# All sixteen gate tiles of a hybrid mLSTM and state-space layer computed in its state-space stage

## The chip, the cores and the metric

The kernel runs on one core of a Trainium2 chip. The core has five engines, each with its own instruction stream, that meet only at semaphores: TensorE (PE, matmuls; PEld is its loading of weights), VectorE (DVE), ScalarE (ACT), GpSimd (POOL) and SyncE (SP), the last two used here mostly to start transfers (DMAs). The metric is the device time of one execution in microseconds (us), as the median of several runs. The times in the rows come from one execution that was recorded by the hardware profiler.

## What is computed

One layer of a diffusion backbone runs over 512 latent tokens and 128 context tokens (640 in all, width 1024). A combined projection feeds an mLSTM (4 heads of width 256, two directions), a state-space branch (S5, 32 groups of 16 channels) and two gates `ga` and `gb`. The two branches are merged under the gates, and a mixture of 16 experts follows. What matters here, cut from the reference:

```python
proj = h @ p['w_in']
q, k, v, o, gates, u, ga, gb = jnp.split(proj, IN_SPLITS, axis=-1)
...
merged = jax.nn.sigmoid(ga) * (h_a @ p['w_pA']) + jax.nn.sigmoid(gb) * (h_b @ p['w_pB'])
out = merged @ p['w_out']
```

`ga` and `gb` are 2048 columns in all. The kernel computes `sigmoid(ga)` and `sigmoid(gb)` as sixteen tiles of 128 columns by 640 tokens.

## The kernel before

The program is a row of stages, each a block in which every engine has its instructions written out in order; at the end of a block all engines meet. The stages are: input and modulation, small projections, the state-space stage, its gated output, the mLSTM, the merge with the output projection, the router, the experts.

**A gate tile.** Tile u is made by `pe_gate` (lines 232 to 241): PE waits for its weights and for the sigmoid of tile u - 1, then runs eight pairs of matmuls, each pair 512 latent and 128 context columns wide (L239, L240), into two PSUM banks. `act_gate` (243 to 249) has ACT take the sigmoid of both banks into a staging row (L248, L249). `store_gate` (251 to 256) has POOL store the row to DRAM (L254) and, behind every odd tile, load the half of the gate weights that comes two halves later (L229). A half is 1 MB and serves two tiles; there are eight halves in two buffers, which are the free tile xT. The merge reads the stored tiles back.

**Where the tiles are.** `NU_S5` (L223) says that tiles 0 to 12 belong to the state-space stage and 13 to 15 to the mLSTM.

**The state-space stage** (blocks up to L950) runs over four quarters q of 8 groups. PE's order is written by hand (L772 on, loop from L776): `lags(q)`, a turn of modulation rows (`pe_ada_turn`, L198), a gate, modulation rows (`pe_ada_rows`, L191), a gate, the coefficients of the next quarter turned (`turn_cb`, L717), a gate, `additions(q + 1, 0)` (L729), `outputs(q)` (L763, L765), `additions(q + 1, 1)`, modulation rows. One more gate stands ahead of the loop. ACT follows in the same order: it copies what PE leaves in PSUM (additions L823 to L826, outputs L864, modulation rows L208, lags L838, turned coefficients L812) and takes the sigmoids between. DVE computes the scan of each quarter (L919 to L944) and the coefficients of the next (L511 to L534).

**The mLSTM** runs over four heads h. PE's order (L1171 on) is `scores(h)` (L1101 to L1116), the projection of the next head's q and k, `values(h)` (L1133, L1143), the projection of the next head's v and o, `turn(h)` (transposes L1155, state update L1166). The last head has no next one; there PE computes tiles 13 and 14 in the first of these places and tile 15 in the second. Beside PE, ACT computes decays (L1216 to L1228), sigmoids, the scaled parts of the values (`inter`, L1237) and, in `finish`, a square root (L1242) and copies; DVE multiplies scores by decays (`weigh`, L1294), combines the values (`combine`, L1303 to L1319), forms the inverse mean square (L1323) and scales the head by its root (L1326), for which PE's transposes wait. Values wait until all five products L1294 are done.

When ACT changes to a function whose table is not loaded, an instruction ACT_TABLE_LOAD stands in front of the activation and bears its line.

Of the kernel before, what the change touches and what calls it, by code (L numbers as in the profile page):

```python
# [27 lines left out]
H, DH = 4, 256  # L28
# [44 lines left out]
def program(nc, ar, out):  # L73
    with ExitStack() as ctx:
# [145 lines left out]


        NU = 16
        NU_S5 = 13  # L223
        gw = xT[:].rearrange("p k t -> p (k t)")[:, 0:4096].rearrange("p (s k n) -> p s k n", s=2, k=KD)
        gstage = [xT[:].rearrange("p k t -> p (k t)")[:, 4096:4096 + TOK], rsb[:]]

# [435 lines left out]
        with ExitStack() as st:  # L662
# [41 lines left out]
            @block.tensor  # L704
            def _(pe):
                gates = iter(range(NU_S5))

                def turn_cb(q, r):

                    if r == 0:  # L710
                        pe.wait_ge(sem("cb_ready"), q + 1)
                        if q:
                            pe.wait_ge(sem("v_copied"), 4 * q)
                    else:
                        pe.wait_ge(sem("ct_copied"), 4 * q + 2)
                    for g in range(QG):
                        mm = pe.transpose(PS[2 + g // 4][:, (g % 4) * P:(g % 4 + 1) * P], CB[:, r, g, :], ident)  # L717
                        if g % 4 == 3:
                            mm.then_inc(sem("cb_turned"), 1)

                def additions(q, r):

                    if r == 0:
                        pe.wait_ge(sem(f"part_in{q}"), 16 * L)
                        pe.wait_ge(sem("ct_copied"), 4 * q + 4)
                    else:
                        pe.wait_ge(sem("v_copied"), 4 * q + 2)
                    for g in range(QG):
                        mm = pe.matmul(PS[2 + g // 4][:, (g % 4) * J:(g % 4 + 1) * J], CT[:, r, g, :],  # L729
                                       U[:, QG * q + g, :], start=True, stop=True)  # L730
                        if g % 4 == 3:
                            mm.then_inc(sem("s5_v_done"), 1)

                def lags(q):

                    pe.wait_ge(sem("ca_ready"), q + 1)
                    pe.wait_ge(sem("bbz_ready"), q + 1)
                    if q:
                        pe.wait_ge(sem("lags_copied"), 4 * q)
                    FW, BW = (L - 1) * GC, 0  # L740
                    for s in range(2):
                        o = s * (2 * L - 1) * GC
                        k = 0
                        for d, (at, m0) in enumerate(((FW, 0), (BW, 1))):
                            for r in range(2):
                                for x in range(4):
                                    g = 4 * s + x
                                    mm = pe.matmul(PS[6][32 * x:32 * x + GC, o + at:o + at + P], bbz[:, d, r, g, :],
                                                   CA[:, r, g, m0:m0 + L, :], start=(k == 0 and s == 0),
                                                   stop=(k == 3), skip_group_check=True)  # L750
                                k += 1
                    mm.then_inc(sem("s5_lag_done"), 1)

                def outputs(q):

                    pe.wait_ge(sem("xp_copied"), q + 1)
                    pe.wait_ge(sem("cao_ready"), q + 1)
                    pe.wait_ge(sem("toeplitz_in"), 128 * (q + 1))
                    if q:
                        pe.wait_ge(sem("z_copied"), 2 * q)  # L760
                    for g in range(QG):
                        dst = PS[g // 4][0:J, (g % 4) * P:(g % 4 + 1) * P]
                        pe.matmul(dst, U[:, QG * q + g, :], T[:, g, :], start=True, stop=False)  # L763
                        for r in range(2):
                            mm = pe.matmul(dst, Xp[:, r, g, :], CAo[:, r, g, :], start=False, stop=(r == 1))  # L765
                        if g % 4 == 3:
                            mm.then_inc(sem("s5_y_done"), 1)

                def gate():
                    pe_gate(pe, next(gates), (4, 5))  # L770

                turn_cb(0, 0)  # L772
                turn_cb(0, 1)
                gate()
                additions(0, 0)
                for q in range(NQ):  # L776
                    lags(q)
                    if q:
                        pe_ada_turn(pe, 3 + 2 * q, 7)
                    else:  # L780
                        additions(0, 1)
                    gate()
                    pe.wait_ge(sem("mod_in"), 4 + 2 * q)
                    pe_ada_rows(pe, 4 + 2 * q, 7)
                    gate()
                    if q + 1 < NQ:
                        turn_cb(q + 1, 0)
                    pe_ada_turn(pe, 4 + 2 * q, 7)
                    if q + 1 < NQ:
                        turn_cb(q + 1, 1)  # L790
                    gate()
                    if q + 1 < NQ:
                        additions(q + 1, 0)
                    outputs(q)
                    if q + 1 < NQ:
                        additions(q + 1, 1)
                    pe.wait_ge(sem("mod_in"), 5 + 2 * q)
                    pe_ada_rows(pe, 5 + 2 * q, 7)
                pe_ada_turn(pe, 11, 7)

            @block.scalar
            def _(act):
# [12 lines left out]
                def additions(q, r):  # L815

                    if q and r == 0:
                        act.wait_ge(sem("xp_copied"), q)
                    for b in range(2):
                        act.wait_ge(sem("s5_v_done"), 4 * q + 2 * r + b + 1)  # L820
                        src = PS[2 + b][:, 0:4 * J].rearrange("p (g j) -> p g j", g=4)
                        gg = slice(4 * b, 4 * b + 4)
                        act.activation(V[F, r, gg, 1:JL + 1], src[F, :, 0:JL], ACT.Copy)  # L823
                        act.activation(V[F, r, gg, JL + 2:NS_], src[F, :, JL:J], ACT.Copy)
                        act.activation(V[B, r, gg, 1:JL + 1], src[B, :, 0:JL][:, :, ::-1], ACT.Copy)
                        act.activation(V[B, r, gg, JL + 2:NS_], src[B, :, JL:J][:, :, ::-1],  # L826
                                       ACT.Copy).then_inc(sem("v_copied"), 1)
# [5 lines left out]
                for q in range(NQ):  # L833
# [27 lines left out]
                    for b in range(2):  # L861
# [3 lines left out]
                                       PS[b][0:J, :].rearrange("p (g i c) -> p g i c", g=4, i=L),  # L865
                                       ACT.Copy).then_inc(sem("z_copied"), 1)
                    if q + 1 < NQ:
                        additions(q + 1, 1)
                    act_ada(act, 5 + 2 * q, 7)

# [143 lines left out]
        with ExitStack() as st:  # L1014
            qk = sb("qk", [P, 2, 4, TOK], F32, st)
# [32 lines left out]
            @block.gpsimd  # L1048
            def _(pool):
                for h in range(H):  # L1050
                    pool.wait_ge(sem("co_ready"), 4 * (h + 1))
                    for d in range(2):
                        pool.dma_start(Cout[h, d], Co[:, 2 * d:2 * d + 2, :]).then_inc(sem("c_out"), 16)
                    if h == H - 2:
                        for u in range(NU_S5, NU):
                            store_gate(pool, u, qk[:, 0, u % 2, :])
                pool.wait_ge(sem("c_out"), 32 * H)

            @block.tensor
            def _(pe):  # L1060
# [110 lines left out]
                for h in range(H):  # L1171
                    scores(h)
                    if h + 1 < H:
                        proj_qk(h + 1)
                    else:
                        for u in range(NU_S5, NU - 1):
                            pe_gate(pe, u, (u % 2, 2))
                    values(h)
                    if h + 1 < H:
                        proj_vo(h + 1)  # L1180
                    else:
                        pe_gate(pe, NU - 1, ((NU - 1) % 2, 2))
                    turn(h)

            @block.scalar
            def _(act):
# [71 lines left out]
                for h in range(H):  # L1258
                    decays(h)
                    if h + 1 < H:  # L1260
                        out_qk(h + 1)
                    else:
                        for u in range(NU_S5, NU - 1):
                            act_gate(act, u, (u % 2, 2), qk[:, 0, u % 2, :])
                    inter(h)
                    if h + 1 < H:
                        out_vo(h + 1)
                    else:
                        act_gate(act, NU - 1, ((NU - 1) % 2, 2), qk[:, 0, (NU - 1) % 2, :])
                    finish(h)  # L1270

            @block.vector
# [718 lines left out]
```

## Time and profile before

| What | Value |
|---|---|
| median of 3 runs | 1861.05 us (1856.96 to 1862.49) |
| profiled execution | 1856.57 us, of which the recorded span is 1854.7 us |
| PE busy | 1689.7 us (91%) |
| DVE busy | 570.0 us (31%) |
| ACT busy | 374.7 us (20%) |
| POOL busy | 100.4 us (5%) |
| mean granted clock of PE over the span | 0.962 |

All times in the rows count from the start of the span. The granted clock is the share of PE's full speed that the chip allowed: 1.00 is 2.4 GHz, 0.50 is 1.2 GHz, and a value between is a stretch that had both. The state-space stage lies between some 110 and 300 us, the mLSTM between 337 and 804, its last head from 733, the merge from 807. A busy PE is not PE at its best; it says only that its instructions follow without a wait.

### The profile page before, as it was taken

Reading aid. Unit: us, or ns where it says so; the run is one execution under the profiler, and the core shown is the slowest. Engines: PE = TensorE matmul, PEld = TensorE weight load, DVE = VectorE, ACT = ScalarE, POOL = GpSimd, SP = SyncE. Lnnn points to the kernel's source line nnn. Section 1 sums busy time; section 2 is a strip of 40 time slices with the busy share of each in tenths; the row PEclk is TensorE's granted clock in tenths of the full one; section 3 lists DMA queues with packets and bytes.
Section 4 is the critical chain, followed back from the end, with each engine's and each line's share of the span. In section 5 each row is a group of like instructions: output and inputs, shape, how many; then the busy total and the mean of one; then the engine's idle time right before and its main releaser. Section 6 shows DMA issues by size and latency. Waiting matters only on the chain. (4 is left out here: it accounts for less than half of the span.)

```text
span 1854.7 us, 33663 instructions
## 1 busy us (share of the span) xinstructions
PE 1689.7 (91%) x15258; PEld 960.7 (52%) x15258; DVE 570.0 (31%) x1313; ACT 374.7 (20%) x777; POOL 100.4 (5%) x95
## 2 busy tenths in 40 slices
PE   5799998999999898968995699999999999999993
PEld 2366665546446464668883234444444444444441
DVE  5369991011213131347646001111111111111113
ACT  3343332121121313145434100000000000000001
POOL 1610000000000000000000000000000000000000
PEclk9799998999999999989998799999999999999997
DMA  9244455010202012043314799999999999999963
GB/s 396 77 110 169 154 182 230 12 46 1 102 12 103 11 47 79 15 157 123 139 69 193 277 355 384 403 401 402 400 403 405 408 404 404 406 400 405 407 255 128
DMA packets 56916, 420.61 MB, mean 227 GB/s; under 512 B 10932, under 2 KB 17588, under 8 KB 26948
## 3 DMA queue, kind: packets, MB, share of 16 engines
q1 hardware_dynamic: 49188, 386.97, 52.7%
q0 software_dynamic: 6864, 28.85, 5.2%
q8 instruction: 120, 1.97, 0.4%
q10 hardware_dynamic: 720, 2.62, 0.3%
q14 instruction: 24, 0.20, 0.0%
HBM read 391.86 MB, written 24.42 MB: 224 GB/s over the span
## 5 line engine op out<-in xcount | busy, mean ns | idle before, releaser
L1737 PE MATMUL bank<-place,x 128*32 128x384 f32 x3120 | 258.1, 489 | 0.9 <-ACT x L1800 0.9
L1737 PE MATMUL bank<-ring_tail,x 128*32 128x384 f32 x3024 | 249.8, 488 | 1.4 <-issue 1.4
L1737 PEld LDWEIGHTS bank<-place,x 128*32 128x32 f32 x3120 | 100.4, 110 | 147.3 <-issue 143.8
L1737 PEld LDWEIGHTS bank<-ring_tail,x 128*32 128x32 f32 x3024 | 98.2, 110 | 145.1 <-issue 143.8
L1831 DVE SCALAR_TENSOR_TENSOR hT<-bank,gvr,xT 32x256 f32<-32x256 f32 (+1 forms) x192 | 92.1, 480 | 241.3 <-PE bank L1767 238.7
L1845 DVE TENSOR_TENSOR hid<-sq,bank 128x384 f32<-128x384 f32 x48 | 23.7, 550 | 446.8 <-issue 362.3
L1089 PE MATMUL bank<-place,hT 128*128 128x512 f32 x320 | 138.0, 592 | 0.0
L239 PE MATMUL bank<-hT,xT 128*128 128x512 f32 x256 | 132.7, 600 | 1.1 <-ACT qk L249 0.9
L1767 PE MATMUL bank<-place,hidT 128*32 128x256 f32 x2304 | 128.0, 379 | 0.0
L1767 PE MATMUL bank<-ring_tail,hidT 128*32 128x256 f32 x2304 | 127.8, 379 | 0.0
L1438 PE MATMUL bank<-a_h,w_h 128*128 128x320 f32 x320 | 101.2, 316 | 19.4 <-DVE w_l L1510 16.9
L1074 PE MATMUL bank<-hT,place 128*128 128x512 f32 x256 | 110.6, 592 | 2.5 <-PEq L952 2.5
L1767 PEld LDWEIGHTS bank<-place,hidT 128*32 128x32 f32 x2304 | 74.0, 110 | 51.3 <-issue 5.0
L1767 PEld LDWEIGHTS bank<-ring_tail,hidT 128*32 128x32 f32 x2304 | 74.3, 110 | 50.7 <-issue 3.3
L1438 PE MATMUL bank<-a_l,w_h 128*128 128x320 f32 x320 | 99.8, 312 | 0.0
L1438 PE MATMUL bank<-a_h,w_l 128*128 128x320 f32 x320 | 99.6, 311 | 0.0
L1089 PEld LDWEIGHTS bank<-place,hT 128*128 128x128 f32 x320 | 60.7, 190 | 74.8 <-issue 74.6
L1818 ACT ACTIVATE hidT<-bank 128x384 f32<-128x384 f32 x48 | 20.1, 491 | 363.6 <-PE bank L1751 363.6
L240 PEld LDWEIGHTS bank<-hT,xT 128*128 128x128 f32 x256 | 48.8, 191 | 61.7 <-issue 61.7
L1074 PEld LDWEIGHTS bank<-hT,place 128*128 128x128 f32 x256 | 48.3, 190 | 62.0 <-issue 62.0
L1438 PEld LDWEIGHTS bank<-a_h,w_h 128*128 128x128 f32 x320 | 60.9, 190 | 22.2 <-DVE w_l L1510 18.1
L1699 POOL DMA_INDIRECT moe_dram<-hT,gidx x16 | 23.1, 1442 | 741.9 <-DVE hT L1831 741.9
(364 smaller groups left out, 1905.4 us busy)
## 6 DMA issues: line engine op xcount, KB each, us to landing
place<-w_e_dram SPq DMA_DIRECT2D x97, 1536.0 KB, 11.6
ring_tail<-w_e_dram SPq DMA_DIRECT2D x95, 1536.0 KB, 11.7
place<-w_ada_dram SPq DMA_DIRECT2D x12, 2048.0 KB, 9.1
xT<-w_gate_dram POOLq DMA_DIRECT2D x8, 1024.0 KB, 6.5
place<-w_qk_dram SPq DMA_DIRECT2D x4, 2048.0 KB, 8.9
place<-w_vo_dram SPq DMA_DIRECT2D x4, 2048.0 KB, 10.7
place<-w_pAB_dram SPq DMA_DIRECT2D x4, 1536.0 KB, 7.9
hT<-gates_dram SPq DMA_DIRECT2D x4, 1280.0 KB, 6.1
```

The costliest lines, as they stand in the source:

```text
L239: pe.matmul(PS[banks[0]][:, :], w, hT[:, k, 0:LAT], start=(k == 0), stop=(k == 7))
L240: mm = pe.matmul(PS[banks[1]][:, 0:CTX], w, hT[:, k, LAT:TOK], start=(k == 0), stop=(k == 7))
L1074: mm = pe.matmul(PS[u % 2][:, :], w, hT[:, k, 0:LAT], start=(k == 0), stop=(k == 7))
L1089: mm = pe.matmul(PS[u % 2][:, :], hT[:, k, t * P:(t + 1) * P], wslot(c)[:, k, :], start=(k == 0), stop=(k == 7))
L1438: mm = pe.matmul(PS[bank][:, 0:TH], wp[:, n % RING, j * P:(j + 1) * P], ap[:, n % RING, x * TH:(x + 1) * TH], start=(k == 0 and i == 0), s ...
L1699: pool.indirect_dma_start(out=ar["moe"][:, :], out_offset=bass.IndirectOffsetOnAxis(ap=gidx[:, e:e + 1], axis=0), in_=ys[:, e % 2, :], in_ ...
L1737: mm = pe.matmul(PS[bank + j][TJ * g:TJ * g + TJ, 0:FC], x[:, e % 2, 2 * c + k, TJ * j:TJ * j + TJ], w[:, k, FC * g:FC * g + FC], start=(c ...
L1767: mm = pe.matmul(PS[y_bank(e) + j // 2][TJ * g:TJ * g + TJ, 256 * (j % 2):256 * (j % 2) + 256], hidT[:, e % 2, j, b * P + TJ * c:b * P + T ...
L1818: ins = act.activation(hidT[:, e % 2, j, :], PS[j][:, 0:FC], ACT.Copy)
L1831: ins = dve.scalar_tensor_tensor(ys[TJ * j:TJ * j + n, e % 2, 256 * g:256 * g + 256], PS[y_bank(e) + j // 2][TJ * g:TJ * g + n, 256 * (j % ...
L1845: ins = dve.tensor_tensor(hid[:, j, :], sl[:, j, :], PS[3 + j][:, 0:FC], ALU.mult)
```

## The change

All sixteen tiles are computed in the state-space stage: `NU_S5` becomes 16, and one more gate stands, on PE and on ACT, behind the outputs of the first, second and third quarter, ahead of the second additions of the next. These three are tiles 4, 8 and 12; the tiles between keep their places and take other numbers. The last mLSTM head loses its three gates on PE and ACT, and POOL its three stores there.

```diff
-        NU_S5 = 13
+        NU_S5 = 16
...
                     outputs(q)
                     if q + 1 < NQ:
+                        gate()
                         additions(q + 1, 1)
                     pe.wait_ge(sem("mod_in"), 5 + 2 * q)
...
                                        ACT.Copy).then_inc(sem("z_copied"), 1)
                     if q + 1 < NQ:
+                        gate()
                         additions(q + 1, 1)
                     act_ada(act, 5 + 2 * q, 7)
...
-                    if h == H - 2:
-                        for u in range(NU_S5, NU):
-                            store_gate(pool, u, qk[:, 0, u % 2, :])
...
                     if h + 1 < H:
                         proj_qk(h + 1)
-                    else:
-                        for u in range(NU_S5, NU - 1):
-                            pe_gate(pe, u, (u % 2, 2))
                     values(h)
                     if h + 1 < H:
                         proj_vo(h + 1)
-                    else:
-                        pe_gate(pe, NU - 1, ((NU - 1) % 2, 2))
                     turn(h)
...
                     if h + 1 < H:
                         out_qk(h + 1)
-                    else:
-                        for u in range(NU_S5, NU - 1):
-                            act_gate(act, u, (u % 2, 2), qk[:, 0, u % 2, :])
                     inter(h)
                     if h + 1 < H:
                         out_vo(h + 1)
-                    else:
-                        act_gate(act, NU - 1, ((NU - 1) % 2, 2), qk[:, 0, (NU - 1) % 2, :])
                     finish(h)
```

## Rows read from the trace of the kernel before

**Rows 1.** Busy time by stretch, one state-space quarter: us, PE, PEld, DVE, ACT, POOL; PEclk, DMA, GB/s

```profile
219.98:264.34 44.36, 44.19 (x307) 29.57 (x306) 40.72 (x92) 17.13 (x39) 3.05 (x5) 1.00 0.53 175
```

**Rows 2.** Waits of PE (125.7 to 301) and DVE (175 to 301): total us, times, longest

```profile
PE bank L717 <- ACT place L812: 0.5, 3, 0.2
...
DVE modT L212 <- PE bank L198: 6.8, 4, 3.7
DVE Kt L914 <- ACT Kt L838: 3.5, 3, 1.2
```

**Rows 3.** Timeline of PE, state-space stage: start, us, line, out<-in, count

```profile
131.29 1.06 PE L239 MATMUL bank<-hT,xT 128*128 128x512 f32 x2
...
140.08 1.92 PE L191 MATMUL bank<-place,cs 128*32 128x512 f32 x16
...
168.82 0.60 PE L765 MATMUL bank<-place,sq 128*80 128x128 f32 x4
169.26 1.91 PE L729 MATMUL bank<-U,place 128*128 128x80 f32 x16
...
174.70 1.05 PE L198 MATMUL bank<-sel,adar 128*128 128x2 f32 x8
...
197.98 1.02 PE L239 MATMUL bank<-hT,xT 128*128 128x512 f32 x2
...
206.63 1.91 PE L729 MATMUL bank<-U,place 128*128 128x80 f32 x16
```

**Rows 4.** Timeline of ACT behind the outputs of the first quarter; idle time in brackets

```profile
170.31 0.38 ACT L823 ACTIVATE place<-bank 64x256 f32<-64x256 f32 x1 [0.26 <-PE bank L729]
...
173.09 0.60 ACT L208 ACTIVATE adar<-bank 128x512 f32<-128x512 f32 x1 [0.78 <-PE bank L191]
```

**Rows 5.** Timeline of DVE, its first instruction on the second quarter's additions

```profile
184.69 0.84 DVE L919 TENSOR_TENSOR tz<-place 128x656 f32<-128x656 f32 x1
```

**Rows 6.** The page's DMA issues: count, KB each, median us to landing

```profile
xT<-w_gate_dram POOLq DMA_DIRECT2D x8, 1024.0 KB, 6.5
```

**Rows 7.** Timeline of PE in the last mLSTM head

```profile
744.32 0.61 PE L1116 MATMUL bank<-qk 128*128 128x128 f32 x4
...
763.25 1.03 PE L1133 MATMUL bank<-C,qk 128*128 128x257 f32 x4
...
780.49 0.70 PE L1143 MATMUL bank<-vt,Pm 128*128 128x257 f32 x2 [0.32 <-DVE nd L1303]
...
789.46 0.38 PE L240 MATMUL bank<-hT,xT 128*128 128x128 f32 x2
793.66 2.36 PE L1155 MATMUL bank<-consts,hacc 128*128 128x128 f32 x10 [3.81 <-DVE hacc L1326]
...
798.07 2.37 PE L1166 MATMUL bank<-vt,place 128*128 128x257 f32 x8 [1.63 <-DVE place L1330]
```

**Rows 8.** Timeline of DVE in the last mLSTM head

```profile
744.52 1.28 DVE L1294 TENSOR_TENSOR Pm<-Pm,bank 128x128 f32<-128x128 f32 x4 [0.83 <-PE bank L1113]
...
786.33 0.19 DVE L1323 RECIPROCAL ssq<-ssq 128x5 f32<-128x5 f32 x1
792.20 1.40 DVE L1326 TENSOR_SCALAR hacc<-hacc,rs 128x256 f32<-128x256 f32 x5 [5.69 <-ACT rs L1242]
```

**Rows 9.** Timeline of ACT in the last mLSTM head

```profile
733.26 1.28 ACT L1223 ACT_TABLE_LOAD   x1
737.48 0.40 ACT L1223 ACTIVATE Pm<-sq,colT 128x128 f32<-128x128 f32 x1 [2.93 <-DVE sq L1282]
...
790.66 1.28 ACT L1242 ACT_TABLE_LOAD   x1
```

**Rows 10.** Busy time by stretch in the last head, columns as in rows 1

```profile
733.30:744.80 11.50, 11.50 (x29) 5.49 (x30) 4.62 (x12) 8.09 (x20) 1.42 (x2) 0.85 0.14 47
...
753.40:754.50 1.10, 0.18 (x2) 0.01 (x1) 0.00 (x0) 0.77 (x2) 0.00 (x0) 1.00 0.00 0
...
795.00:796.00 1.00, 1.00 (x6) 1.00 (x5) 0.00 (x0) 0.99 (x4) 0.00 (x0) 0.50 0.00 0
```

## The prediction

> **What bounds the kernel now.** On the page TensorE (PE) is the busiest engine, but that is a mean over stages with different limits, so I read it stage by stage, and only the two stages that the change touches.
>
> First the busy time by stretch over one quarter of the state-space stage. The reader is to see a quarter of 44.36 us with PE busy for 44.19 of it and VectorE (DVE) for 40.72, at a granted clock of 1.00 [rows 1]. Two engines are nearly full, so the next view asks which waits for which. In the list of waits PE's largest entry is 0.5 us in three waits on ScalarE (ACT), while DVE waits 6.8 us in four for PE's line 198 and 3.5 us in three for the lag tables that follow PE's lags [rows 2]. So **PE is the bound of a quarter**, with DVE some 2 us behind.
>
> Then the timeline of PE, DVE and ACT in the last mLSTM head, where the other three gate tiles are now. The reader is to see three places: PE's first values matmul at 763.25, its transposes at 793.66, and what each was waiting for [rows 7 to 9]. Around them the head's path is scores, DVE's weighing, values, DVE's combining, ACT's square root, DVE's scaling, transposes.
>
> **The state-space stage: three gates more.** A gate is eight pairs of matmuls. The one at 197.98 is followed by additions at 206.63: 8.65 us [rows 3]. The one at 131.29 is followed by other work at 140.08: 8.79 us [rows 3]. The new gates stand between the outputs (last matmul group at 168.82) and the second additions (169.26) [rows 3], where PE now stands still for nothing, so nothing there hides them. I take the row that is also followed by additions: 3 x 8.65 = **+25.95 us**, with 3 x 8.79 = 26.37 as the upper end. PE's waits in this stage could at most vanish, which puts the lower end 0.5 lower, at 25.4.
>
> Does a new wait come with them? Everything behind the new gate moves together by 8.65, so I look at what runs beside it.
> - ACT gets two sigmoids between its copies of the outputs and its copies of the second additions. The gate's PE wait on the sigmoid before it is long met, since a whole set of outputs lies between. The copies of the additions start at 170.31, 1.05 behind the additions at 169.26, and ACT's copy of the modulation row starts behind them at 173.09, while PE asks for that row at 174.70 [rows 3, 4]. The existing gate at 197.98 has the same neighbours (sigmoids, then copies of additions) and PE does not wait there. Cost taken: nothing; without this cover a sigmoid pair late by its own length, some 0.9 us, in each of three quarters.
> - DVE takes the additions up only at 184.69 [rows 5], 11 us behind ACT's last copy, so it does not notice. DVE's other work of the quarter gets 8.65 us more room.
> - GpSimd (POOL) stores each tile and, behind odd tiles, loads the weights two halves ahead. A half lands in a median of 6.5 us [rows 6], and two whole gates, 17.3 us, lie between its request and its use. The new tiles are numbers 4, 8 and 12, even ones, so in their places only a store is added; the odd ones keep gates on both sides. SyncE's weight loads wait for the same PE steps as before. Cost taken: nothing.
>
> **The last head: three gates less.** Two lie between scores and values. The scores end at 744.32 + 0.61 = 744.93 [rows 7]. Values need all five products of DVE; the last ends at 744.52 + 1.28 = 745.80 [rows 8]. From DVE's end to PE's start I take what the transposes show: scaling ends at 792.20 + 1.40 = 793.60, PE starts at 793.66, so 0.06 [rows 7, 8]. Values then start at 745.86 instead of 763.25: **17.39 us gained** of the two gates' 18.3 or so; what is late next is DVE's last product, 0.93 us behind the scores. If DVE's end were not the last, the scores' end would be the limit, 0.93 better.
>
> The third gate follows the values (last group at 780.49, ending 781.19) and ends at 789.46 + 0.38 = 789.84 [rows 7]. It is on the path for another reason: ACT must do its sigmoids, then load the square root's table (790.66, 1.28 us), before DVE scales at 792.20, although DVE had the mean squares ready at 786.33 + 0.19 = 786.52 [rows 8, 9]. Without it that table is loaded behind ACT's last copy for the values, while DVE still combines: a table load does not wait for its operand, as the one at 733.26 shows, 4.2 us ahead of the first exponential at 737.48 [rows 9]. DVE then scales 0.06 + 0.26 = 0.32 behind 786.52, where 0.06 is the handoff above and 0.26 is 792.20 less the table load's end at 791.94: 786.84. That is **5.36 us gained**; with the table load in the way, 4.08.
>
> Together 22.75 us; ends 17.39 + 4.08 = 21.5 and 22.75 + 0.93 = 23.7. So of three gates (25.95 us) just some 3.2 us was ever hidden in the head, and 22.75 stood on its path. The modules behind it (copies of the state, its store, the merge) follow in the same order.
>
> Here the Trainium skill speaks against the change: "Perfetto Trace Analysis", section Optimization Strategy, says that where the most-contended engine changes from stage to stage, interleaving the stages may pay, which means keeping filler where PE waits for others. By it the three gates were free and the sum would be +26; by the rows above it is +3.2.
>
> **The clock.** PE now stands still from 789.84 to 793.66, and the clock is already 0.50 for the transposes [rows 7, 10]. Afterwards it stands still from 763.80 to about 770.9 (both ends shifted by their gains), 7.1 us. The transposes cost the same, since they are at half clock today. The eight state-update matmuls behind them take 2.37 us [rows 7]. Should the clock still be down for them too, they lose between nothing and their own length, 2.4 us; I take **+0.4**, near to nothing, because a part of that time is waits for ACT to copy the first four away. Ahead of the values the wait is 0.93 us. In the run of before, between the first two gates of this head, PE was busy for only 0.18 of 1.10 us and the clock stayed at 1.00 [rows 10].
>
> **Sum.** +25.95 - 22.75 + 0.4 = **+3.6 us**; ends +25.4 - 23.7 = +1.7 and +26.37 - 21.5 + 2.4 = +7.3. The profiled execution took 1856.57 us (span 1854.7), so it would become 1860.2; it lies 4.5 us under the median of the three runs. On the median the forecast is 1861.05 + 3.6 = **1864.6**.
>
> **Rivals.**
> - *The values run cold (slower).* The scores of this head spent part of their time at half clock: 0.85 over 11.5 us is 2 x 0.15 x 11.5 = 3.45 us at half [rows 10]. The gates behind them are dense work. Values without them could meet another such stretch: half of 3.45 lost, 1.7 us, giving 1866.4; two stretches give 1868.1; all 17.9 us at half give +18, 1882. It decides from 2.0 us lost, 4 us at half more than today. For it: the longer standstill behind, and a clock that fell in this head already. Against: the scores end and the values begin at 1.00, and 0.92 us without work left it there. The Trainium skill ("TensorE: Matmul & The Clock Gate", section on HAM oscillation) says that a PE that pauses between bursts of work falls to half rate and pays when it returns; the turn of the head agrees (0.50), the short wait does not.
> - *A quarter gets a new wait (slower).* If sigmoids, store or a weight load came late in each of three quarters, 0.9 to 2 us each: +2.7 to +6, 1867 to 1871. Against: the slack of 1.6 us or more in each row above.
> - *The gates of the head were free after all (slower).* +26, 1887. It needs something other than DVE's product at 745.80 to hold the values; I see none.
> - *The quarters hide gates (faster).* Were PE's row padded and DVE the true bound, a quarter of DVE's 40.72 plus its short gaps could take in a gate. One of three hidden gives 1856, still about equal; two give 1847. For it: DVE's load. Against: DVE waits for PE in every quarter, not the reverse [rows 2].
> - *The change does nothing in the head*, values starting no earlier: the same +26 as above.
>
> **How the numbers follow.** About 0.3%, 5.6 us, is what a measurement of this kernel can tell from no change. Forecast, within that: 0.68. Cold values or turn beyond it: 0.19; new waits: 0.07; free gates: 0.01; hidden gates: 0.05. So faster 0.05, same 0.68, slower 0.27. The range takes the low end of the sum on the lower runs, 1856.96 + 1.7 = 1858.7, and reaches up past its high end on the median, 1868.4, to the two cold stretches and the new waits: 1858.5 to 1870.
>
> **What would show it.** Each of the first three quarters 8.65 us longer, PE without a wait over 0.5 us in it; values of the last head about 1 us behind the scores; a square-root table load ahead of the mean squares; transposes some 25 us behind the first values matmul (before: 30.4); the merge about 3.6 us later than now. Wrong would be a PE wait behind a new gate, or a granted clock under 0.9 while the values run.

## The result, and the profile after

The changed kernel takes 1873.17 us (median of 7 runs, 1868.9 to 1879.47) against 1861.05 (7 runs, 1856.96 to 1869.51): ratio 1.0066, 95% interval 1.0041 to 1.009. It is **slower by 12.1 us**, where +3.6 was forecast. The profiled execution took 1870.34 us (before: 1856.57).

Where the difference lies, from the two profiled executions:

| Stretch | before, us | after, us | difference | forecast |
|---|---|---|---|---|
| start to the first gate | 116.3 | 116.7 | +0.4 | 0 |
| first gate to the mLSTM's first projection | 221.0 | 247.8 | +26.8 | +25.95 |
| from there to the last head's scores | 396.0 | 399.0 | +3.0 | 0 |
| last head, start of its scores to its transposes | 60.4 | 37.6 | -22.7 | -22.75 |
| transposes to the merge's first matmul | 15.9 | 17.2 | +1.3 | +0.4 |
| merge | 155.5 | 160.4 | +4.8 | 0 |
| the rest | | | +0.2 | 0 |

The two large terms came out as forecast. Some 9 us came from three stretches whose work the change does not touch. The view of busy time by stretch shows what differs in them (us, then busy us of PE, PEld, DVE, ACT and POOL with their instructions, granted clock of PE, DMA share, GB/s). After: a quarter with its new gate, the three projecting heads, the values, the wait ahead of the last head's transposes, its turn (transposes, state update and the way to the merge), the merge, and the merge's first 5.7 us once more:

```profile
185.05:238.07 53.02, 52.84 (x341) 34.41 (x337) 40.71 (x92) 17.88 (x40) 3.57 (x6) 1.00 0.45 154
364.50:763.50 399.00, 379.59 (x1205) 207.73 (x1205) 70.39 (x221) 77.48 (x185) 2.86 (x4) 0.97 0.13 46
776.04:794.10 18.06, 17.57 (x76) 13.99 (x76) 10.58 (x36) 5.09 (x9) 0.00 (x0) 1.00 0.00 1
794.10:801.10 7.00, 0.00 (x0) 0.00 (x0) 6.25 (x22) 0.21 (x1) 0.00 (x0) 0.69 0.00 0
801.13:818.32 17.19, 6.66 (x20) 4.65 (x20) 2.09 (x5) 6.13 (x15) 1.42 (x2) 0.50 0.15 40
818.32:978.70 160.38, 150.06 (x959) 147.68 (x960) 101.70 (x186) 69.07 (x126) 0.00 (x0) 0.95 0.36 134
818.30:824.00 5.70, 5.68 (x21) 5.68 (x22) 3.04 (x6) 1.69 (x4) 0.00 (x0) 0.50 1.00 383
```

The kernel before, the heads, the turn, the merge, and the merge's first 4.7 us:

```profile
337.30:733.30 396.00, 376.60 (x1205) 206.39 (x1205) 70.44 (x221) 77.53 (x185) 2.87 (x4) 0.98 0.13 47
793.66:809.56 15.90, 5.05 (x20) 3.71 (x20) 2.09 (x5) 6.12 (x15) 1.44 (x2) 0.72 0.15 43
809.56:965.10 155.54, 145.23 (x959) 142.83 (x960) 101.73 (x186) 69.07 (x126) 0.00 (x0) 0.99 0.37 139
809.50:814.20 4.70, 4.64 (x17) 4.64 (x18) 2.15 (x5) 1.65 (x4) 0.00 (x0) 0.50 0.99 375
```

The reader is to see that the counts are equal but for a record, that time without PE work in the merge is equal (160.38 - 150.06 = 10.32; 155.54 - 145.23 = 10.31), and that **only PE's busy time grew, where its granted clock fell**: 0.72 to 0.50 in the turn, 0.99 to 0.95 in the merge, 0.98 to 0.97 in the heads. No new wait appeared in these three stretches.

The timeline of PE after shows the places (start, us, line, out<-in, count, idle time before and what ended it):

```profile
774.51 0.61 PE L1115 MATMUL bank<-qk 128*128 128x128 f32 x4
776.04 1.14 PE L1132 MATMUL bank<-C,qk 128*128 128x257 f32 x4 [0.93 <-DVE Pm L1283]
...
801.13 2.39 PE L1154 MATMUL bank<-consts,hacc 128*128 128x128 f32 x10 [7.05 <-DVE hacc L1315]
...
805.58 3.84 PE L1165 MATMUL bank<-vt,place 128*128 128x257 f32 x8 [1.63 <-DVE place L1319]
818.32 0.64 PE L1427 MATMUL bank<-a_h,w_h 128*128 128x320 f32 x1 [8.90 <-DVE w_l L1499]
...
845.55 0.31 PE L1427 MATMUL bank<-a_h,w_l 128*128 128x320 f32 x1
848.45 0.63 PE L1427 MATMUL bank<-a_h,w_h 128*128 128x320 f32 x1 [2.59 <-DVE w_l L1499]
848.88 0.47 PE L1427 MATMUL bank<-a_l,w_h 128*128 128x320 f32 x1
```

The same pause of the merge in the timeline before:

```profile
836.29 0.31 PE L1438 MATMUL bank<-a_h,w_l 128*128 128x320 f32 x1
839.18 0.41 PE L1438 MATMUL bank<-a_h,w_h 128*128 128x320 f32 x1 [2.58 <-DVE w_l L1510]
839.43 0.30 PE L1438 MATMUL bank<-a_l,w_h 128*128 128x320 f32 x1
```

PE now stands still for 7.05 us ahead of the transposes (3.81 before [rows 7]). The clock falls within that wait (0.69 over it) and is not back until the merge is 5.7 us old: the state update takes 3.84 us instead of 2.37 [rows 7]. The kernel before began its merge at half clock too, for 4.7 us, so most of the merge's +4.8 us comes from its three pauses: all three end at half clock after and at full clock before, the first of them although it is equally long (2.59 and 2.58 us; matmuls of 0.47 us instead of 0.31 behind it).

### The profile page after: what moved, and what is told of

It reads as the page before. It is cut to its first block and busy times, and to the rows that moved or that the text cites. A ratio compares the mean times of both kernels' runs of the same rounds, so it can differ in the third digit from the quotient of the medians.

```text
span 1868.5 us, 33662 instructions
## 1 busy us (share of the span) xinstructions
PE 1700.0 (91%) x15258; PEld 967.8 (52%) x15258; DVE 568.7 (30%) x1313; ACT 373.4 (20%) x776; POOL 100.2 (5%) x95
## 5 line engine op out<-in xcount | busy, mean ns | idle before, releaser
L1427 PEld LDWEIGHTS bank<-a_l,w_h 128*128 128x128 f32 x320 | 62.9, 197 | 0.0
```

What stands on the lines that cost most here:

```text
L1427: mm = pe.matmul(PS[bank][:, 0:TH], wp[:, n % RING, j * P:(j + 1) * P], ap[:, n % RING, x * TH:(x + 1) * TH], start=(k == 0 and i == 0), s ...
```

## The experiments

**The theory:** the 9 us beyond the working sum are PE at half clock, and they follow from taking dense work out of the last head. **The rivals:** the gates cost more in the state-space stage than the profile of one execution says; or the halved stretches fall where chance puts them, and the parts of the change would show no such loss.

All runs, with the mean granted clock over all executions of each kernel. In these sessions the kernel before took 1860.8 to 1861.3 us.

| Kernel | median, us (range; runs) | ratio to before [95%] | clock |
|---|---|---|---|
| before, the four later sessions | 1861.2 (1856.59 to 1873.3; 86) | | 0.954 |
| the change (first session) | 1873.17 (1868.9 to 1879.47; 7) | 1.0066 [1.0041, 1.009] | 0.949 |
| a_again: the change | 1873.69 (1871.15 to 1877.78; 7) | 1.0065 [1.004, 1.009] | 0.947 |
| head_only | 1847.87 (1844.26 to 1848.85; 6) | 0.9917 [0.989, 0.9944] | 0.947 |
| s5_only | 1888.57 (1885.69 to 1902.8; 6) | 1.0155 [1.0119, 1.0191] | 0.954 |
| fill_turn | 1878.44 (1875.63 to 1878.83; 6) | 1.0085 [1.0058, 1.0112] | 0.949 |
| fill_turn7 | 1866.04 (1861.95 to 1876.98; 11) | 1.003 [1.001, 1.0049] | 0.955 |
| delay_merge | 1870.95 (1865.05 to 1875.87; 6) | 1.0047 [1.003, 1.0063] | 0.949 |
| a_fill | 1867.44 (1862.21 to 1876.97; 12) | 1.0043 [1.0026, 1.0061] | 0.955 |
| b_fill | 1859.74 (1854.56 to 1868.1; 11) | 0.9994 [0.9976, 1.0012] | 0.958 |
| a_heads | 1857.58 (1855.31 to 1859.26; 12) | 0.9972 [0.996, 0.9985] | 0.963 |
| b_heads | 1854.55 (1853.94 to 1856.98; 11) | 0.996 [0.9945, 0.9975] | 0.963 |
| a_three | 1862.93 (1858.65 to 1866.32; 12) | 1.0003 [0.9989, 1.0017] | 0.958 |
| b_three | 1857.92 (1852.92 to 1862.61; 12) | 0.9972 [0.9956, 0.9988] | 0.960 |

b_again and head_again are one execution each of the kernel before and of head_only: 1865.8 and 1839.58 us; the latter lies 4.7 us under the fastest of head_only's six. fill_turn7 had a twelfth execution, of 4597.91 us, which no run explains and which is left out.

### The parts of the change alone

**a_again** is the changed kernel once more, beside the others.

> The changed kernel once more, to see how much of its extra time is the same in every execution. Theory work: the added and removed work is +3.2 us net, and the rest of the measured +12 us is chance, so some executions come within 5 us of the kernel before. Theory clock: the change costs some 8 us more through stretches at half clock in the last head and the merge, so all executions stay 8 us or more above the kernel before, and the trace shows half clock at the merge's pauses again.

The slowdown stands: 1873.69 us. Busy time by stretch, its turn and merge:

```profile
805.84:822.91 17.07, 6.67 (x20) 4.66 (x21) 2.09 (x5) 6.13 (x15) 1.42 (x2) 0.50 0.15 40
822.91:981.90 158.99, 148.68 (x959) 146.28 (x960) 101.72 (x186) 69.07 (x126) 0.00 (x0) 0.96 0.36 136
```

**head_only** takes the three gates out of the last head and adds none elsewhere: tiles 13 to 15 are not computed, tiles 10 to 12 are stored a second time in their places. The edit is to the kernel after.

```diff
-        NU_S5 = 16
+        NU_S5 = 13
...
+                    if u >= 10:
+                        pool.dma_start(ar["gates"][u + 3], gstage[u % 2]).then_inc(sem(f"gate_out{u % 2}"), 16)
...
-                        gate()
                         additions(q + 1, 1)
```

> The last head without its three gate tiles, and the state-space stage with thirteen as before; tiles 13 to 15 are not computed, copies of tiles 10 to 12 are stored in their place. Theory work: -22.75 us against the kernel before, 1838. Theory clock (the standstill in the head costs time behind it): the head itself gains 22.7, but the state update runs 1.5 us longer and the merge several us, so only -13 to -17 us, 1844 to 1848.

In the median of six executions, taking the gates away saved **13.0 us, not 22.75** (the single head_again, below, saved more). Its heads, turn and merge by stretch:

```profile
338.50:742.10 403.60, 384.32 (x1205) 209.76 (x1205) 70.42 (x221) 77.51 (x185) 2.86 (x4) 0.95 0.12 46
779.70:796.52 16.82, 6.67 (x20) 4.66 (x20) 2.08 (x5) 6.13 (x15) 1.42 (x2) 0.50 0.15 41
796.52:955.80 159.28, 148.96 (x960) 146.57 (x960) 101.75 (x186) 69.09 (x126) 0.00 (x0) 0.96 0.36 135
```

From the start of the last scores to the merge's end this execution takes 955.80 - 742.10 = 213.7 us, the kernel before 965.10 - 733.30 = 231.8: 18.1 saved. So 4.7 of the missing 9.8 are in the turn and the merge, at the clock seen in the change. By the medians the other 5 then lie ahead of the last scores, where PE's program in the heads is that of before; in this execution they took 403.6 us instead of 396.0.

**s5_only** is the change with three gates computed again in the last head (into the same staging rows, not stored): the state-space half of the change alone.

```diff
                     if h + 1 < H:
                         proj_qk(h + 1)
+                    else:
+                        for n in range(2):
+                            pe_gate_again(pe, n, (n % 2, 2))
                     values(h)
                     if h + 1 < H:
                         proj_vo(h + 1)
+                    else:
+                        pe_gate_again(pe, 2, (0, 2))
                     turn(h)
```

> All sixteen tiles in the state-space stage as in the changed kernel, and the last head keeps three gate tiles' work too: it computes tiles 13 to 15 a second time and stores none of them. Theory work: +25.95 us against the kernel before, 1887. Theory clock in the head: the same +26, since the head and the merge are as before. A rival, that the extra 8 us come from the state-space stage: +34, 1895.

It costs +27.7 us for 25.95 of work, at the clock of the kernel before (0.954): to within some 2 us the gates are not dearer in the state-space stage. Its heads, turn and merge by stretch:

```profile
364.00:764.20 400.20, 381.08 (x1205) 208.56 (x1205) 70.46 (x221) 77.51 (x185) 2.86 (x4) 0.97 0.12 46
824.46:841.18 16.72, 6.52 (x20) 4.51 (x20) 2.09 (x5) 6.13 (x15) 1.42 (x2) 0.51 0.16 41
841.18:996.50 155.32, 144.99 (x960) 142.59 (x960) 101.72 (x186) 69.09 (x126) 0.00 (x0) 0.99 0.37 139
```

With the gates back in the last head the merge is back at 155.3 us, although its turn ran at 0.51. By the medians the parts add up to the change within their scatter (27.7 - 13.0 = 14.7 against 12.1 and 12.9), and **the loss belongs to the half that was forecast as pure gain**.

### The turn of the last head and the merge

**fill_turn** and **fill_turn7** put matmuls that nobody reads (128x512, into a free bank) ahead of the last transposes, 14 and 7 of them.

```diff
                     if h + 1 < H:
                         proj_vo(h + 1)
+                    else:
+                        for _ in range(14):
+                            pe.matmul(PS[2][:, :], hT[:, 0, 0:P], hT[:, 0, 0:LAT], start=True, stop=True)
                     turn(h)
```

> The changed kernel, with fourteen matmuls of 128x512 that nobody reads on PE ahead of the last head's transposes, some 6 us of work in a wait of 7.05 us. Theory work: no change against the changed kernel, 1873. Theory clock: the transposes and the state update of this head run at full clock, 2 to 2.5 us less, and more if the merge then meets fewer stretches at half clock: 1863 to 1871.

> As fill_turn, but with seven matmuls: each 128x512 matmul stands in the trace as two records and takes 0.86 us, so fourteen were 12 us and held the transposes back by 4.8 us; seven are 6.0 us and fit the wait of 7.05. Theory clock in the turn: transposes and state update at full clock, 2.5 us less than the changed kernel, about 1871. Theory that the merge's pauses matter more than the turn: between 1864 and 1872, by whether the clock still falls at the merge's pauses.

fill_turn was sized wrongly by me: such a matmul takes 0.86 us here, two records of 0.43, so 14 of them fill 12 us of a 7 us wait, and the transposes came 4.8 us late; 1878.44 us mixes a gain with that price. Still, its transposes ran at full clock, 1.25 us instead of 2.39, as PE's timeline shows:

```profile
810.09 1.25 PE L1154 MATMUL bank<-consts,hacc 128*128 128x128 f32 x10
```

Its merge was as slow as in the change all the same (by stretch):

```profile
826.22:986.40 160.18, 149.85 (x959) 147.44 (x960) 101.73 (x186) 69.07 (x126) 0.00 (x0) 0.95 0.36 135
```

fill_turn7 fits the wait (6.0 us) and took 1866.04 us, **7 us less than the change, with more work in it**. That is the median; the two intervals overlap, and the executions fall into two groups, seven at 1862 to 1867 us and four at 1873 to 1877. The profiled one (1874.46) is of the upper group, with 407.6 us in its heads. Its heads, turn and merge by stretch:

```profile
363.80:771.40 407.60, 388.38 (x1206) 212.58 (x1207) 70.52 (x221) 78.81 (x185) 4.12 (x6) 0.94 0.12 45
811.11:827.02 15.91, 5.17 (x20) 3.52 (x20) 2.09 (x5) 5.92 (x15) 1.42 (x2) 0.72 0.16 44
827.02:982.70 155.68, 145.36 (x960) 142.96 (x960) 101.76 (x186) 69.09 (x126) 0.00 (x0) 0.98 0.37 138
```

Turn and merge are as long as in the kernel before (15.90 at 0.72, 155.54), the turn by coincidence: here the transposes ran at full clock and the state update at half, before it was the other way round (2.36 and 2.37 us [rows 7]). The gain expected in the state update did not come. PE's timeline:

```profile
811.11 1.31 PE L1154 MATMUL bank<-consts,hacc 128*128 128x128 f32 x10 [1.05 <-DVE hacc L1321]
...
814.86 3.64 PE L1165 MATMUL bank<-vt,place 128*128 128x257 f32 x8 [2.21 <-DVE place L1325]
```

**delay_merge** is the change with two more copies on ACT, some 1.5 us, ahead of the merge's first step, so that the merge starts later against whatever went before.

```diff
+                    if n == 0:
+                        for _ in range(2):
+                            chain(act, "act")(act.activation(a_h[:, 0, :], a_raw, ACT.Copy))
```

> The changed kernel, with two more copies on ACT ahead of the merge's first step (written twice over into the same place), some 1.6 us of pure delay. Theory work: 1.6 us slower than the changed kernel, 1875. Theory of the merge's start: the clock rises at the same moment as without the delay, so the merge has less work at half clock behind it, 4.1 us instead of 5.7, as in the kernel before (4.6), and its pauses then fall where the clock holds: half clock at 845 to 900 goes, 4.8 us, so 1869 to 1871 although 1.6 us were added.

It took 1870.95 us, some 2.7 less than the change, though it only adds a delay; the two intervals overlap, so the sign rests on the trace. The profiled execution was the slowest of the six (1875.87, with 407.0 us in the heads). In it the turn, still at 0.50, is 1.4 us longer than in the change, and the merge 4.8 us shorter:

```profile
809.65:828.26 18.61, 6.66 (x20) 4.65 (x20) 2.09 (x5) 7.59 (x17) 1.42 (x2) 0.50 0.22 62
828.26:983.80 155.54, 145.24 (x959) 142.82 (x960) 101.76 (x186) 69.08 (x126) 0.00 (x0) 0.99 0.36 136
```

So a turn at half clock does not by itself make a slow merge (s5_only shows the same), and transposes at full clock do not make a fast one (fill_turn). In nearly all traces one mark goes with the slow merge: the clock came up 5.5 to 6.2 us behind the merge's first matmul where the pauses then cost clock (the change, a_again, fill_turn, head_only, and below head_again and a_three), and 4.0 to 4.8 us behind where they did not (before, s5_only, fill_turn7, delay_merge, and below b_three). b_again, below, breaks it: the clock came up after 3.3 us, and two of the three pauses still cost clock. So the mark does not decide it; what does stays open.

**a_fill** and **b_fill** are the kernels after and before, with unread matmuls ahead of and behind the last turn, at the merge's start and in its three pauses. The edit of a_fill; in b_fill the seven are three, behind the last gate's sigmoid:

```diff
+                    else:
+                        idle(pe, 7)
                     turn(h)
+                idle(pe, 4)
...
+                idle(pe, 7, 3)
...
+                    if kind == "A" and k == 0 and m:
+                        pe.wait_ge(sem("branch_used"), 8 * (m - 1) + 1)
+                        idle(pe, 0, 3)
```

> The changed kernel, with matmuls that nobody reads in PE's waits from the last head's transposes on: seven (6.0 us) ahead of the transposes, four (3.5 us) behind the state update, three of 384 columns (1.9 us) ahead of the merge's first step and in each of its three pauses between columns. Theory clock: no work of the merge at half clock at its pauses, 4.8 us, and 2.5 us in the turn: 1864 to 1867, less where the merge also starts at full clock. Theory work: no change, 1873.

> The kernel before, with the same matmuls in the same waits (three, 2.6 us, ahead of the transposes, since the wait there is 3.8). Theory clock: 1 us in the transposes, 0 to 2.3 at the merge's start: 1857 to 1860; the difference to a_fill is then the net of the work alone, 3.2 us. Theory work: 1861, and a difference of 12 to a_fill.

The change gains 6.2 us by it (1873.69 to 1867.44), the kernel before 1.5, so 4.7 of the difference sits there; 7.7 us are left between the two, where 3.2 had been expected if only the work were left. The executions of each spread over some 14 us, so these shares are rough. Merges by stretch, a_fill:

```profile
815.80:969.80 154.00, 149.47 (x980) 144.38 (x978) 100.91 (x185) 68.47 (x124) 0.00 (x0) 1.00 0.37 139
```

and b_fill:

```profile
819.70:974.90 155.20, 150.68 (x979) 145.74 (x978) 100.80 (x185) 68.47 (x124) 0.00 (x0) 0.99 0.37 137
```

### The first three heads

**a_heads** and **b_heads** put unread matmuls into the waits of all four heads' turns as well; **b_again** and **head_again** are one execution more of the kernel before and of head_only.

```diff
+                    idle(pe, 2)
                     pe.wait_ge(sem("kw_ready"), h + 1)
...
                     if h + 1 < H:
                         proj_vo(h + 1)
+                        idle(pe, 4)
```

> a_fill, and in addition matmuls that nobody reads in the waits of all four turns: four (3.5 us) ahead of the transposes of the first three heads, two (1.7 us) behind the transposes of each head. If stretches at half clock in the heads make the spread and a part of the difference, this kernel is several us faster than a_fill (1867) and its executions lie closer together: 1855 to 1862. If not, 1867 as a_fill.

> b_fill with the same matmuls in the turns. Theory clock: with PE kept at work in both kernels, only the work is left between them, so a_heads is 3 to 4 us slower than this one, which comes to 1852 to 1858. If something else than the clock costs the changed kernel its 8 us, the difference stays at 8 to 12.

> The kernel before once more, one look: its profiled execution (1856.57) was among its fastest. If the merge of the kernel before always starts so that its pauses hold the clock, the merge takes 155.5 us here too, and what differs between executions is the heads (397.6 us in the first profile). If the merge's length is chance, it may be 159 to 160 here, as in the kernels without gates in the last head.

> head_only once more, one look (tiles 13 to 15 not computed). If the missing gates set where the merge starts against the clock, its merge takes 159 us again and half clock lasts from the standstill ahead of the transposes into the merge, 27 us; if that was chance, 155.5 and shorter stretches.

With the clock kept up in both (0.963 and 0.963), the kernels are 1857.58 - 1854.55 = **3.03 us apart: about the +3.2 us of work that the prediction had worked out** from the rows of before. The match to two tenths is partly luck: the executions of each spread over 3 to 4 us, and the two profiled ones still differ by 2.3 us in the heads. And b_heads beats both kernels: 1854.55 us, 0.996 [0.9945, 0.9975] of before. Heads by stretch, a_heads:

```profile
364.90:760.00 395.10, 389.71 (x1241) 210.40 (x1242) 70.42 (x221) 76.93 (x185) 2.87 (x4) 0.99 0.13 47
```

and b_heads:

```profile
338.30:731.10 392.80, 386.76 (x1241) 208.85 (x1241) 70.40 (x221) 76.93 (x185) 2.86 (x4) 1.00 0.13 47
```

More matmuls, less time: 1241 records in 392.8 us against 1205 in 396.0 and more. The two single executions show how far the unfilled heads and merge wander. b_again:

```profile
339.30:739.30 400.00, 380.71 (x1204) 208.63 (x1204) 70.44 (x221) 77.48 (x185) 2.86 (x4) 0.96 0.13 46
799.70:817.00 17.30, 6.56 (x21) 4.55 (x21) 2.12 (x5) 6.16 (x15) 1.43 (x2) 0.50 0.14 40
817.00:974.90 157.90, 147.59 (x959) 145.21 (x960) 101.66 (x186) 69.09 (x126) 0.00 (x0) 0.97 0.36 137
```

and head_again, heads and merge:

```profile
336.80:732.80 396.00, 376.61 (x1204) 206.44 (x1204) 70.43 (x221) 77.47 (x185) 2.87 (x4) 0.98 0.13 47
...
787.40:946.40 159.00, 148.70 (x960) 146.30 (x960) 101.67 (x186) 69.05 (x126) 0.00 (x0) 0.96 0.36 136
```

So the kernel before can have a turn at 0.50 too; its merge was then 157.9, between the two cases. The same program's heads took 396.0 or 400.0 us, head_only's 403.6 or 396.0. This qualifies the result of head_only: head_again stands 21.7 us under the median of before (1861.32), close to the 22.75 of the work alone. Against the profiled execution of before, whose heads are equally long, it saved 17.0; so with equal heads 5.8 us of the forecast gain are lost, 4.5 of them in the turn and the merge (16.90 and 159.00 against 15.90 and 155.54).

**a_three** and **b_three** fill only the first three heads' turns and leave the last head and the merge as they are.

```diff
+                    if h + 1 < H:
+                        idle(pe, 2)
                     pe.wait_ge(sem("kw_ready"), h + 1)
...
                         proj_vo(h + 1)
+                        idle(pe, 4)
```

> The changed kernel, with matmuls that nobody reads in the waits of the first three heads' turns alone (four ahead of the transposes, two behind them); the last head, its turn and the merge are those of the changed kernel. If the first three heads carry a part of the 12 us, this kernel stands some 8 us over b_three: 3 of work and 5 of the last turn and the merge. If they carry none, 12 us over it.

> The kernel before with the same matmuls in the first three heads' turns alone. With the first three heads alike in both kernels, the difference to a_three is what the work, the last turn and the merge cost together: 8 us by the stages of the traces, 12 us if the first heads have no share.

They are 1862.93 - 1857.92 = 5.0 us apart, less than either figure expected (8 and 12). Less the 3.0 of work, 2 us belong to last turn and merge by the medians. The traces, a_three's heads, turn and merge,

```profile
364.00:759.00 395.00, 389.61 (x1241) 210.28 (x1241) 70.43 (x221) 76.93 (x185) 2.86 (x4) 0.99 0.13 47
795.50:812.20 16.70, 6.69 (x21) 4.69 (x21) 2.12 (x5) 6.17 (x15) 1.42 (x2) 0.60 0.16 42
812.20:972.40 160.20, 149.89 (x959) 147.49 (x960) 101.69 (x186) 69.04 (x126) 0.00 (x0) 0.95 0.36 135
```

and b_three's merge,

```profile
805.60:961.30 155.70, 145.39 (x960) 142.99 (x960) 101.71 (x186) 69.11 (x126) 0.00 (x0) 0.98 0.37 139
```

put 4.5 there in the merge alone. The other 7 us of the 12.1 vanish when the first three heads are filled: that gains the change 10.8 us (1873.69 to 1862.93) and the kernel before 3.3.

**The account of the 12 us:** 3.0 work; 2 to 5 the last turn and the merge; the rest, 4 to 7, half clock that goes away when the first three heads are filled. That what goes beyond the work is PE's clock is shown to about a microsecond by a_heads and b_heads. That the missing gates of the last head lengthen the merge is shown by the traces of the kernels that have no filler and no delay in the last head or at the merge: 159.0 to 160.4 us in all five without the gates (the change, a_again, head_only, head_again, a_three), 155.3 to 157.9 in all four with them (before, b_again, s5_only, b_three). **What stays open** is the share of the first three heads, and whether the change brings it at all: their code is the same in all kernels and runs ahead of the place that was changed, and the profiled stages (unfilled heads from 396.0 to 403.6 us without the new gates ahead, from 399.0 to 407.6 with them, and 400.2 in s5_only) scatter as much as that share is large. Half clock falls in them for some 3 us at a time or for up to 20 in one piece, as here around the turn of the first in fill_turn7 (busy time by stretch):

```profile
534.00:551.00 17.00, 13.29 (x31) 7.96 (x32) 3.97 (x11) 5.53 (x13) 1.44 (x2) 0.53 0.09 31
```

Which of these an execution gets, no experiment here tells.

## Why the prediction was right or wrong, point by point

- **Three gates in the state-space stage, +25.95: right.** The quarter is 53.02 us long, 44.36 [rows 1] and 8.66. DVE's margin, put at some 2 us, is 3.6 by the same rows (44.36 - 40.72), which changes nothing in the sum. No new wait: over the same part of the stage PE's longest entry in the list of waits after is the same as in [rows 2],

```profile
PE bank L717 <- ACT place L813: 0.5, 3, 0.2
```

  and s5_only measured 27.7 for the whole half. The rival of a new wait is out, and so are hidden gates.
- **Values 17.39 us earlier: right.** They start 1.53 us behind the start of the last group of scores instead of 18.93 [rows 7]: 17.40, held by DVE's product as named (idle 0.93).
- **Transposes 5.36 us earlier: right** (25.09 behind the first values matmul instead of 30.41 [rows 7]: 5.32). The square root's table is loaded ahead of its operand, as read from [rows 9]. The timeline of ACT after, table load,

```profile
792.82 1.28 ACT L1236 ACT_TABLE_LOAD   x1
```

  and of DVE, inverse mean square and scaling:

```profile
799.21 0.19 DVE L1312 RECIPROCAL ssq<-ssq 128x5 f32<-128x5 f32 x1
799.67 1.41 DVE L1315 TENSOR_SCALAR hacc<-hacc,rs 128x256 f32<-128x256 f32 x5 [0.28 <-ACT rs L1236]
```

- **Free gates, or a change without effect in the head: out** (head_only 0.9917 [0.989, 0.9944] of before).
- **The clock, +0.4: wrong; this is the step that failed.** It came to some 9 us. The standstill was forecast to a tenth (7.1; 7.05), and a doubled state update was the upper bound (2.4), but the sum took 0.4, "near to nothing", on the ground that waits for ACT would cover it; it was +1.47. The larger part was not priced at all: the step looked eight matmuls ahead and stopped at the end of the head. Half clock lasted from some 4 us ahead of the transposes through the first 5.7 us of the merge, with PE busy for just 6.66 of the 17.19 us between, and then came back at the merge's three pauses. [rows 10] had shown 0.50 at 795 in the kernel before; the rows behind it, where the clock recovered at 797, fell again and came back 4.7 us into the merge, were not read. The rest of the 9 us (4 to 7 by the medians, 3.0 in the profiled pair) is half clock in the first three heads, at which the step did not look either; why the change has more of it there stays open.
- **Cold values: right cause, wrong place.** The values ran at 1.00, as the 0.92 us row suggested. That rival's prices for one and two stretches, 1866.4 and 1868.1, were also short.
- **The merge itself was left out of the sum.** "The merge about 3.6 us later" was 8.8 in the profiled pair, 3.0 of it from the first three heads, and the merge grew by 4.8.
- **Interleaving.** The Trainium skill ("Perfetto Trace Analysis", section Optimization Strategy) says that interleaving regimes with different most-contended engines may pay. The prediction weighed that as +26 or nothing. By the runs it lies between: of 25.95 us of filler the head hid 3.2, but taking it away saved 13.0 in the median (17.0 with equal heads), not 22.75. The time that filler hides and the clock that it keeps up are two terms, and here the second was the larger.
- **The clock's fall in a pause.** The Trainium skill ("TensorE: Matmul & The Clock Gate", section on HAM oscillation) says that a PE that pauses between bursts of work falls to half rate. The turn agrees (0.50 after 7.05 us without work). The merge's pauses bear it out in part only: 2.59 us without work ended at half clock after the change, 2.58 at full clock before it.

The range ended at 1870 for the same reason: the sum's bound for the clock was the 2.4 us of one state update, and the rival's two stretches of 3.45 us were the most that was taken beyond it.

## What to carry to other kernels

Where a stage has filler in its waits, ask two prices of moving it: the time that it hides, and the clock that it keeps; follow the granted clock behind the emptied wait until a long dense stretch has brought it back, into the next stage and its pauses. Matmuls that nobody reads, sized from the trace to end before the wait does, are a cheap test of the second price, and may be worth keeping (before: 1861.3 to 1854.55 us). Compare two kernels with the clock kept up in both when the question is which has less work.

## What the runs showed of the hardware

- Half clock outlasted the wait in which it began by far (the change): granted 0.50 over all of 17.19 us in which PE was busy for 6.66, and then over 5.7 us of dense matmuls.
- Pauses of one length (2.6 us) cost clock in some kernels and not in others, and even in two executions of one kernel (before: merges of 155.54 and 157.90 us). In the one execution profiled with a delay of 1.4 us ahead the merge was 4.8 us shorter.
- The scatter of this kernel is mostly clock: with the waits filled the runs of the change lie within 4.0 us (a_heads) instead of 10.6, those of the kernel before within 3.0 (b_heads) instead of 12.6. Unfilled heads of 396.0 us stood at a mean of 0.98, those of 407.6 at 0.94.
- One 128x512 matmul of this type is two records, 0.43 us each at full clock (fill_turn: 28 records for 14 matmuls, 12.18 us).
